# A fused transformer block on one core: late modulation columns summed by single-column products in half precision, from accumulators that GpSimd splits

## The reference

```python
silu_c = jax.nn.silu(c)
mod_l = (silu_c @ w_mod[l] + b_mod[l])[:, None, :]          # 1024 -> 6 * 1024
sh1, sc1, gt1, sh2, sc2, gt2 = jnp.split(mod_l, 6, axis=-1)
pl = modulate(rms_norm(xl, g_mix[l]), sh1, sc1) @ w_in[l]   # Hyena, GQA and neighbourhood columns
...
mix_l = jnp.concatenate([hyo_l, gqa_l, na_l], axis=-1) @ w_out[l]
xl = xl + gt1 * mix_l
xl = xl + gt2 * swiglu(modulate(rms_norm(xl, g_ffn[l]), sh2, sc2), w_ffn_in[l], w_ffn_out[l])
return rms_norm(xl, g_final)
```

## Time and profile before

| | |
|---|---|
| median of 3 executions | 1250.49 us (1248.52 to 1252.25) |
| span of the profiled execution | 1246.6 us |
| PE busy | 1226.5 us (98%) |
| DVE busy | 979.6 us (79%) |
| ACT, POOL busy | 653.0 us (52%), 398.3 us (32%) |
| granted clock, mean | 0.998 |

### The profile page before, as it was taken

How to read it: one execution, slowest core, us unless ns; L and a number is a source line. 1 busy time by engine, 2 the same in 40 slices (tenths; PEclk the granted TensorE clock), 3 DMA queues, 4 the chain that set the end, 5 groups by cost and what they waited for, 6 DMA issues and landing times. The chain is left out here.

```text
span 1246.6 us, 22702 instructions
## 1 busy us (share of the span) xinstructions
PE 1226.5 (98%) x8085; PEld 668.1 (54%) x8085; DVE 979.6 (79%) x1597; ACT 653.0 (52%) x1231; POOL 398.3 (32%) x385
## 2 busy tenths in 40 slices
PE   7999999999999999999999999999999999999998
PEld 1564656556775666664454555554555554444444
DVE  3879998676778999964479888888888885666587
ACT  2642234556779999963145554455555543412425
POOL 0000000114678988850320444445554430000001
PEclk9999999999999999999999999999999999999999
DMA  9728723235210130121300332322223307997963
GB/s 354 282 87 318 260 78 136 68 87 155 67 35 2 35 136 9 29 86 51 118 34 1 102 102 84 92 85 66 87 90 101 101 28 265 336 339 249 351 228 135
DMA packets 111043, 164.35 MB, mean 132 GB/s; under 512 B 8560, under 2 KB 70000, under 8 KB 109552
## 3 DMA queue, kind: packets, MB, share of 16 engines
q1 hardware_dynamic: 110960, 163.24, 38.5%
HBM read 138.57 MB, written 22.55 MB: 129 GB/s over the span
## 5 line engine op out<-in xcount | busy, mean ns | idle before, releaser
L1327 PE MATMUL PS<-arena 128*128 128x512 f16 (+9 forms) x7485 | 1185.2, 319 | 13.1 <-DMA arena<-in_w_mod 5.7
L1327 PEld LDWEIGHTS PS<-arena 128*128 128x128 f16 (+3 forms) x7485 | 617.3, 100 | 555.3 <-issue 33.5
L3133 DVE SCALAR_TENSOR_TENSOR arena<-arena 128x512 f16<-128x512 f32 x128 | 111.6, 878 | 30.6 <-ACT arena L2361 29.8
L2361 ACT ACTIVATE arena<-arena 128x512 f16<-128x512 f32 x120 | 75.4, 631 | 103.2 <-PE PS L1327 103.2
L2491 ACT ACTIVATE arena<-arena 128x512 f16<-128x512 f32 x77 | 48.1, 629 | 124.7 <-DVE arena L3354 74.6
L3017 DVE TENSOR_REDUCE arena<-PS 128x1 f32<-128x512 f32 (+1 forms) x160 | 106.8, 680 | 3.3 <-PE PS L1327 3.3
L1321 POOL TENSOR_TENSOR arena<-arena 128x1 f32<-128x1 f32 x8 | 4.7, 598 | 231.3 <-DVE arena L3521 227.9
L2262 ACT ACTIVATE arena<-PS 128x512 f16<-128x512 f32 x125 | 75.7, 605 | 2.8 <-PE PS L1327 1.8
L1171 POOL TENSOR_TENSOR arena<-arena 128x512 f16<-128x512 f32 x64 | 74.0, 1158 | 8.0 <-ACT arena L2265 5.4
L3190 DVE TENSOR_TENSOR arena<-PS,arena 128x256 f32<-128x256 f32 (+1 forms) x100 | 55.2, 553 | 25.9 <-PE PS L1327 25.6
L3369 DVE SCALAR_TENSOR_TENSOR arena<-arena 128x512 f16<-128x512 f32 x77 | 52.2, 687 | 18.9 <-ACT arena L2491 18.8
(11 more groups left out here) (227 smaller groups left out, 1321.0 us busy)
## 6 DMA issues: line engine op xcount, KB each, us to landing
arena<-in_w_ffn_out SPq DMA_DIRECT2D x121, 256.0 KB, 5.2
arena<-in_w_mod SPq DMA_DIRECT2D x23, 1024.0 KB, 7.2
arena<-in_w_ffn_in SPq DMA_DIRECT2D x88, 256.0 KB, 3.0
left_operands<-arena SPq DMA_DIRECT2D x43, 256.0 KB, 2.9
arena<-in_w_in SPq DMA_DIRECT2D x9, 1024.0 KB, 5.6
arena<-left_operands SPq DMA_DIRECT2D x3, 2816.0 KB, 12.1
arena<-lay_bias SPq DMA_DIRECT2D x12, 512.0 KB, 3.9
arena<-in_x SPq DMA_DIRECT2D x2, 2048.0 KB, 14.1
```

Of the source, the lines that this page charges most:

```text
L1327: return pe.matmul(out, lhsT, rhs, start=start, stop=stop, skip_group_check=True)
L2361: act.activation(block_split(p, b)[:, 0], weight_block(p, b, first), ACT.Copy, scale=WS).then_inc(blk_hi, 1)
L3133: dve.scalar_tensor_tensor(dst[:, 1], src, WS, dst[:, 0], ALU.mult, ALU.subtract).then_inc(blk_lo, 1)
```

## The change

GpSimd takes over a step between VectorE's accumulation and TensorE's sums.

- The factor of the late rows is `silu_s`, which is `silu(c)` times 256 (`WS`), made by one VectorE instruction at the start, behind a wait for `silu_rdy`. The accumulators are thereby 256 times as large.
- For each group GpSimd waits for the group's eight rows, copies `macc[g]` to half precision (`late_hi`) and writes the difference to the accumulator as a second half (`late_lo`), into new buffers `mhalves[g]`. Groups 0, 1 and 2 stand in its queue behind the wait for all transposes of `x` (`hT_mm` 20) and ahead of its first inverse root for the projections; `late_hi(3)` stands after the inverse root of unit 16, `late_lo(3)` after that of unit 17.
- `late_columns` waits for the split and not for the rows. It takes sixteen half-precision products in place of eight float32 ones: for each 128 features the high and the low half, added up in PSUM.
- `late_sum` multiplies by 1/256 as it adds the bias.

```diff
+            def late_hi(g):
+                pool.wait_ge(late_used, 8 * g + 8)
+                own.step(pool.tensor_copy(mhalves[g][:, 0], macc[g]))
+
+            def late_lo(g):
+                own.wait()
+                pool.tensor_tensor(mhalves[g][:, 1], macc[g], mhalves[g][:, 0], ALU.subtract).then_inc(late_split, 1)
+
+            pool.wait_ge(hT_mm, 20)
+            for g in range(3):
+                late_hi(g)
+                late_lo(g)
...
                 inverse_roots(u)
+                if u == GROUP0[0] - 4:
+                    late_hi(3)
+                if u == GROUP0[0] - 3:
+                    late_lo(3)
...
             def late_columns(g, bank):
 
-                pe.wait_ge(late_used, 8 * g + 8)
+                pe.wait_ge(late_split, 2 + g + 1)
                 for i in range(8):
-                    ins = mm(PS[:, bank, 8 * g + i:8 * g + i + 1], macc[g][:, i * P:i * P + P], ones1, True, True)
+                    for part in range(2):
+                        ins = mm(PS[:, bank, 8 * g + i:8 * g + i + 1], mhalves[g][:, part, i * P:i * P + P], ones16[:, 0:1],
+                                 part == 0, part == 1)
                 ins.then_inc(late_mm, 1)
...
+            dve.wait_ge(silu_rdy, 1)
+            own.step(dve.tensor_scalar(silu_s, silu_c[:, :, 0], WS, None, ALU.mult))
...
-                acc, s = macc[g], silu_c[:, 2 * kp + i, 0:1]
+                acc, s = macc[g], silu_s[:, 2 * kp + i:2 * kp + i + 1]
...
-                dve.tensor_tensor(mod[:, 16 + 8 * g:24 + 8 * g, 0], PS[:, (6, 7, 3, 5)[g], 8 * g:8 * g + 8],
-                                  cols[:, V_BMOD + 16 + 8 * g:V_BMOD + 24 + 8 * g], ALU.add).then_inc(late_rdy, 1)
+                dve.scalar_tensor_tensor(mod[:, 16 + 8 * g:24 + 8 * g, 0], PS[:, (6, 7, 3, 5)[g], 8 * g:8 * g + 8], 1 / WS,
+                                         cols[:, V_BMOD + 16 + 8 * g:V_BMOD + 24 + 8 * g], ALU.mult, ALU.add)\
+                    .then_inc(late_rdy, 1)
```

More of the change, by code:

```diff
@@ L447, in build @@
         ones1 = f32(2.1875, 1)
+        ones16 = f16(2.19140625, 2)
         warm = f32(2.19921875, 1)
+        silu_s = f32(3.25, 8)
         ssq = f32(2.25, 2, 8)
@@ L489, in build @@
         macc = [f32(o, GW) for o in (Z, Z + 4, Z, Z + 8)]
+        mhalves = [f16(o, 2, GW) for o in (Z + 67, Z + 71, Z + 75, Z + 12)]
         decay = f32(Z + 24, NT + 1, HYW)
@@ L599, in build @@
         late_used = sem("late_product_added")
+        late_split = mrow_rdy
         late_mm = sem("late_group_by_feature")
@@ L1124, in _ @@
             own.step(pool.memset(half1, 0.5))
+            own.step(pool.memset(ones16, 1.0))
             own.wait()
```

## The result

The changed kernel takes 1255.75 us (median of 4 runs, 1254.58 to 1256.09) where the one before takes 1249.51 on the same chip: 6.2 us more, a ratio of 1.0045 with a 95% interval of 1.003 to 1.006. The forecast was 8.5 us more.

What follows compares the result with a forecast made beforehand. PE, busy 1226.5 of 1246.6 us, was taken as the bound, with VectorE as critical up to 172.49 us. PE's 6.0 us lateness plus 2.5 us of clock made 8.5; 1250.5 + 8.5 = 1259.0 us, range 1250.0 to 1263.0.

Steps and rivals of the forecast that it cites:

- the forecast's own part: Whole run: the time if the forecast's course holds, GpSimd durations and clock at their likely ends, 1257 to 1263 us; chance 0.54.
- rival 2: Group 1: copy runs beside `lo_of`, or GpSimd keeps its turn; PE 2.5 us late, 1253.5 to 1256.0 us; chance 0.20.
- TensorE's saving: Late groups on PE: 16 half-precision products take 0.46 us, saving 1.24 us per group, 5.0 us in all.
- GpSimd's own time: Split of each group: copy 1.22 us and difference 2.32 us, from doubled 512-wide durations; 3.5 us per group.
- Turns: Group 1: GpSimd's copy and difference alternate with the two `lo_of`, one whole instruction each, the difference ending at 137.55 us.
- The signs: Changed trace, group 1: GpSimd's two operations stretched by 2.2 us or more, a `lo_of` of some 3.5 us.
- The wait: Before the second late group: PE stands 8.4 us for GpSimd's difference; `turn_v(0)` starts 6.0 us late.
- The clock: After PE stands at group 1: about 5 us of work at half speed, costing 2.5 us; bounds nothing and 10 us.
- Rope scaling and the wait behind it: Group 2: GpSimd's difference holds the first rope scaling back 1.25 us; PE waits for L2923, losing its 1.24 us gain.
- Rival 1: Group 1: `lo_of` doesn't hold GpSimd, halves ready at 132.75, PE 1.15 us late; 1250.4 us, not slower; chance 0.15.
- Rival 3: All four late groups: sums are only shorter, 5.0 us less, 1245.5 us; chance 0.06.
- Rival 4: After group 1: clock stays low until `turn_v(3)` is through, 6.0 + 10 us, 1266.5 us; chance 0.05.

Runs made afterwards that it cites:

- the run without reads: The changed kernel, but GpSimd fills group 1's halves with zeros by memset, not reading the accumulator: 1249.65 us, ratio 0.9995 to the kernel before.
- the run put around VectorE's chain: The changed kernel with GpSimd's group 1 start, second late group, late_sum(1), chunk 9's rows and rope scaling moved later: 1244.81 us, ratio 0.9966 to before.

## Why the prediction was right, step by step

**What the number alone says.** 1255.75 us is inside the range, but below the forecast's own part of it (1257 to 1263) and inside what rival 2 allowed (1253.5 to 1256.0). Counted from the time before, 6.2 us is still a little under the 6.5 us at which the forecast's own part began. So the time doesn't decide between the two; the trace does, as below. The steps are right in kind and in place, and nearly every size was taken too large.

**TensorE's saving.** A group of 16 half-precision products takes 0.40 us (25 ns each) and not 0.46: in the first late group all sixteen lie in the stretch from 119.40 to 119.82, beside one product of 512 columns.

```profile
L1349 PE MATMUL PS<-arena 128*128 128x1 f16 x16 | 0.5, 163 | 0.0
```

The saving is 1.30 us and not 1.24. It arrives at group 3 in full and at group 2 not at all, as forecast.

**GpSimd's own time.** Doubling a 512-wide operation counted its fixed part twice: 1.04 and 2.13 us, not 1.22 and 2.32. By the two widths (0.61 against 1.04, 1.16 against 2.13) that part is an estimated 0.2 us of each.

**Turns.** Right in order and place, the copy included: it waits for `lo_of` with its one operand too, which ends the second rival. The Trainium skill (SBUF — State Buffer, "Who interferes with whom") says that a VectorE instruction with two SBUF inputs contends with a GpSimd instruction that reads SBUF, and not with one that only writes it. The trace agrees: the copy takes 3.03 us against 1.04, and the memsets, which only write, aren't held up. The signs were a little weaker than named: the copy and the difference were stretched by 2.0 and 1.9 us and not by 2.2 or more, and the longer `lo_of` takes 3.1 us and not 3.5. The subtraction of group 0 held VectorE's product back by 0.7 us (1.92 against 1.23), forecast 1.05, and most of it went into the pause behind it: the rows of group 1 end 1.16 us later than before, 0.15 more than the head's 1.0 where 0.6 was forecast.

**The wait.** 8.4 us forecast, 7.1 by the trace. The sizes above make the difference: the rows end 0.4 us earlier than forecast, and the four turns behind them take 7.2 us (130.2 to 137.4) and not 7.95. `turn_v(0)` starts at 137.9 where it was 132.1: 5.8, less the 1.0 of the head 4.8 us late where 6.0 was forecast. This is the term that was mis-sized most.

**The clock.** 5 us at half speed and 2.5 us of cost were forecast from bounds of 0 and 10; some 4.8 us at 1.2 GHz are seen, and the run with TensorE kept at work gets 2.0 us back. That the 5 us came so close is luck. They were twice a fall of 1.3 to 3.3 us read off the end of the run, but here PE stands from 130.4 on and the clock falls only at 135.4; and the prediction had no row for a rise. By `lo_of_v(3)` (150.48 against 142.71 before) VectorE is 7.8 less 1.0, 6.8 us late: 4.8 and 2.0 for the clock.

**Rope scaling and the wait behind it.** 3.38 us against 2.62: 0.76, forecast 1.25, since GpSimd's copy and subtraction are shorter. Where PE waits was named only in part: 1.3 of its 2.0 us fall ahead of `project(2)`, for `scale` (L2910), and 0.7 ahead of `turn_qk(0)`, for L2950, the L2923 of before. The chain of work on VectorE that it waits for is the one named.

**The end.** 6.8 + 0.76 - 1.36 = 6.2 us (6.8 behind `lo_of_v(3)`, 0.76 of the rope scaling, 1.36 gained at group 3 as measured with that group alone), which is what the medians show. Rival 1 (no turns) is refuted by the trace, and the run without reads shows what it would have given: no change. Rival 3 needed more than shorter sums; its 5.0 us were reached as 4.1 only when GpSimd's start, the place of the second late group and VectorE's order were changed as well. Rival 4 didn't come about.

## What to carry to other kernels

When a helper engine is put between two others, ask for each of its instructions what the neighbours run at that moment: here a GpSimd read beside VectorE instructions with two SBUF operands cost both engines time (2.0 us of a copy, 0.8 us of a `lo_of`), and beside ones with an operand from PSUM nothing. A saving on the busiest engine counts only where no other engine is as late; before it is built, follow the other chain to the point where they meet next. And a wait on TensorE can cost more than its length: here the one of 7.1 us cost over a quarter more (2.0 us), because the clock stayed at 1.2 GHz for some 4.8 us of work behind it.

## What the runs showed that was not expected

Near 294 us, in the attention on neighbours, PE stands without a releaser that the view can name (1.5 us before). Over the profiles of nearly the same program this time goes from 0.2 us (the run put around VectorE's chain) to 3.0 us (group 2 alone split, where the view names a VectorE instruction that had itself stood), and after the long ones the clock falls for some microseconds (there 0.59 and 0.56 in 298 to 302 us). VectorE and ScalarE stand as well. Spans of single profiles can differ by several microseconds for this and the head alone, so the verdicts above rest on the medians. Its cause was not looked for.

The narrow products hardly feel the clock: 16 of them took 0.40 us at 2.4 GHz (group 0) and 0.44 at 1.2 GHz (137.47 to 137.91).
